# Asking for the third expert's weights as soon as the order of experts is known

## The reference, cut to what matters

```python
def moe_ffn(h, router_w, router_bias, w_gate, w_up, w_down):
    ...
    _, idx = lax.top_k(jnp.where(in_group, sel, -jnp.inf), TOP_K)
    ...
    for e in range(N_EXPERTS):
        he = jax.nn.silu(h @ w_gate[e]) * (h @ w_up[e])
        y = y + gates[..., e:e + 1] * (he @ w_down[e])
    return y
```

## Time and profile before

| | |
|---|---|
| median of 3 runs | 1428.83 us |
| lowest and highest | 1424.74, 1430.57 us |
| profiled execution | 1431.29 us |
| its span, first to last instruction | 1429.5 us |
| granted tensor engine clock, mean | 0.881 of full |
| PE busy | 1155.3 us (81%) |
| DVE busy | 459.9 us (32%) |
| ACT busy | 265.1 us (19%) |
| DMA moved | 344.03 MB, mean 241 GB/s |

### The profile page before, as it was taken

How to read it: one execution, slowest core, us unless ns; L and a number is a source line. 1 busy time by engine, 2 the same in 40 slices (tenths; PEclk the granted TensorE clock), 3 DMA queues, 4 the chain that set the end, 5 groups by cost and what they waited for, 6 DMA issues and landing times.

```text
span 1429.5 us, 15764 instructions
## 1 busy us (share of the span) xinstructions
PE 1155.3 (81%) x5976; PEld 566.9 (40%) x5976; DVE 459.9 (32%) x1107; ACT 265.1 (19%) x588; POOL 122.2 (9%) x107
## 2 busy tenths in 40 slices
PE   4899978888989469999895499977799399985554
PEld 1363433444654223333332347533478233322223
DVE  2321355764742601111111511356762401110013
ACT  1320101223520401111111412100241211100002
POOL 2000031820000100000000200034100100000001
PEclk8899999979899779999998699997579699997776
DMA  9612106739995489999999410005001599999972
GB/s 347 227 64 113 59 0 241 297 132 413 375 354 209 166 311 381 393 396 389 394 418 400 171 51 9 0 23 213 0 1 59 202 374 383 397 410 416 426 322 92
DMA packets 86997, 344.03 MB, mean 241 GB/s; under 512 B 6918, under 2 KB 42187, under 8 KB 64395
## 3 DMA queue, kind: packets, MB, share of 16 engines
q1 hardware_dynamic: 67056, 308.76, 55.6%
q10 hardware_dynamic: 15867, 20.77, 4.3%
q0 software_dynamic: 4000, 13.49, 2.6%
HBM read 300.92 MB, written 42.07 MB: 240 GB/s over the span
## 4 chain that ended last, share of the span: by engine, by line
PE 64%; DMA 17%; DVE 11%; ACT 3%; issue 2%; POOL 1%; ACTq 1%; SPq 1%; POOLq 0%; DVEq 0%
PE ps L888 15%; PE ps L502 12%; DMA ring<-in_exp_w_up 10%; PE ps L911 7%; PE ps L790 6%; PE ps L511 5%; PE ps L445 4%; DMA ring<-in_w_mod 3%; PE ps L467 3%; DMA arena<-in_exp_w_up 2%; PE ps L769 2%; PE ps L687 2%; PE ps L667 2%; PE ps L739 1%; DMA arena<-slots,slot_ids 1%
## 5 line engine op out<-in xcount | busy, mean ns | idle before, releaser
L888 PE MATMUL ps<-ring,arena 128*32 128x256 f32 (+1 forms) x1344 | 198.7, 532 | 44.0 <-DMA ring<-in_exp_w_up 44.0
L445 PE MATMUL ps<-cst,arena 128*128 128x128 f32 x558 | 100.6, 311 | 95.9 <-DMA arena<-slots 37.2
L502 PE MATMUL ps<-u,ring 128*128 128x512 f32 (+1 forms) x416 | 166.9, 561 | 9.8 <-ACT u L1729 4.0
L1587 DVE TENSOR_TENSOR arena<-arena,ps 128x128 f32<-128x128 f32 (+1 forms) x59 | 27.0, 499 | 379.3 <-ACT arena L1885 379.3
L445 PEld LDWEIGHTS ps<-cst,arena 128*128 128x128 f32 x558 | 69.7, 158 | 177.2 <-issue 58.4
L888 PEld LDWEIGHTS ps<-ring,arena 128*32 128x32 f32 (+1 forms) x1344 | 70.6, 136 | 155.2 <-issue 114.7
L502 PEld LDWEIGHTS ps<-u,ring 128*128 128x128 f32 x416 | 79.6, 193 | 94.6 <-issue 89.6
L888 PE MATMUL ps<-arena 128*64 128x512 f32 (+1 forms) x544 | 84.1, 536 | 24.6 <-DMA arena<-in_exp_w_up 24.6
L911 PE MATMUL ps<-arena 128*32 128x256 f32 (+1 forms) x672 | 93.4, 482 | 1.6 <-ACT arena L1894 1.6
L790 PE MATMUL ps<-u,ring 128*128 128x512 f32 (+1 forms) x256 | 85.3, 495 | 2.3 <-DVE h L1421 1.3
L511 PE MATMUL ps<-ring,u 128*128 128x256 f32 (+1 forms) x224 | 76.6, 502 | 7.7 <-DVE arena L1240 7.7
(11 more groups left out here) (285 smaller groups left out, 1203.3 us busy)
## 6 DMA issues: line engine op xcount, KB each, us to landing
ring<-in_w_mod SPq DMA_DIRECT2D x24, 2048.0 KB, 11.6
ring<-in_exp_w_gate SPq DMA_DIRECT2D x22, 2048.0 KB, 23.3
ring<-in_exp_w_up SPq DMA_DIRECT2D x22, 2048.0 KB, 27.0
arena<-in_exp_w_down SPq DMA_DIRECT2D x22, 2048.0 KB, 21.3
slots<-zeros SPq DMA_DIRECT2D x4, 6144.0 KB, 42.5
arena<-in_exp_w_gate SPq DMA_DIRECT2D x10, 2048.0 KB, 24.0
arena<-in_exp_w_up SPq DMA_DIRECT2D x10, 2048.0 KB, 29.5
u<-in_exp_w_down SPq DMA_DIRECT2D x10, 2048.0 KB, 26.5
```

Of the source, the lines that this page charges most:

```text
L445: return nc.tensor.transpose(dst, src, ident[0:n, 0:n])
L502: last = nc.tensor.matmul(bank[row:row + width, 0:T - c0], w[:, k, n:n + width], u[:, k, c0:T], start=(k == 0), stop=(k == KT - 1))
L888: last = nc.tensor.matmul(ps[n * part:n * part + n, 2 + b % 2, 0:2 * width].rearrange("p (s n) -> p s n", s=2), x_k, pair[:, :, a:a + widt ...
```

## The change

After the wait for the order and the passes, gate and up of place 2 are asked for at once. Then SyncE waits for `ut_taken` and asks for down of place 2. Then it waits for the scatter and asks for down of place 1. The wait for block 1's rows (`x_landed1`) is gone. From place 3 on nothing changes.

```diff
                     sp.wait_ge(S("order_ready"), l + 1)
                     sp.wait_ge(S("passes_ready"), l + 1)
-                    sp.wait_ge(S("scattered", l), 32 * (TT - FIRST_T[l]))
-                    sp.wait_ge(S("x_landed1", l), 16 * (P // expert_blocks(l)[1][3]))
                     nc.sync.reg_load(passes_left, passes[0:1, l:l + 1])
                     nc.sync.reg_add(passes_left, passes_left, 1)
-                    load_down(1, 1)
                     for o, r in list(enumerate(rank_order(l)))[FIXED:]:
                         e = nc.sync.value_load(order[0:1, r:r + 1], min_val=0, max_val=NE - 1)
                         load_gate_up(o, e)
+                        if o == FIXED:
+                            sp.wait_ge(S("ut_taken"), ut_count(l, TT - 1, 1) + 1)
                         load_down(o, e)
+                        if o == FIXED:
+                            sp.wait_ge(S("scattered", l), 32 * (TT - FIRST_T[l]))
+                            load_down(1, 1)
```

## The result

The changed kernel takes 1457.47 us (median of 4 runs, 1453.31 to 1459.85) against 1429.7 us for the kernel before in the same comparison: ratio 1.0187, 95% interval 1.0163 to 1.0211. It is 27.8 us slower by the medians, 26.7 by the ratio, which isn't their quotient. The forecast was 1439 with a range from 1427 to 1446: the side was right, the size was not.

The account below looks back on a forecast made before the run. Both expert stages were taken to end when the last weights land, with DMA engines full and later asks waiting for the tensor engine. Layer 0 +13.4 and layer 1 -3.3 gave +10.1 us on the 1428.83 median: 1439, range 1427 to 1446.

Parts of the forecast that it names:

- the turns that the scatter waits: Weight packets sent ahead of remaining scatter packets on each DMA engine: scatter 13.3 us later in layer 0, 3.8 in layer 1.
- the tokens: Token loads of blocks 0 and 1 meeting queued weights: 3.2 us more in layer 0, 9.7 for 3.4 in layer 1.
- the slack of the start: Layer 0: second token pair landed 1.2 us before its transpose, so 1.2 us was taken off the start's delay.
- the stock: Queued weight loads covering a late tensor engine at the thinnest ask: 1.9 us in layer 0, 10.5 in layer 1.
- a start more than 20 us late in layer 0: Last listed case, the tensor engine starting over 20 us late in layer 0; chance 0.05.
- the ceiling of the gain: Most the early asks could bring: 1.9 us in layer 0 plus 4.8 in layer 1, 6.7 us.
- marks named in the prediction: Expected profile signs: asks near 498 and 1132, scatter wait ending near 521 and 1139.5, layer 0's last load 13 us later.
- the ratio of 1.67 packets of the scatter for one of the weights: DMA engine sharing, from 157 software queue packets beside 94 of q1: 49 scatter packets let 29 weight turns pass.
- Case C: Rival, scatter and weight packets one for one: +15.1 us in layer 0, +12.5 together, 1441; chance 0.55 shared with the forecast.
- the prediction's own row of two hardware queues: Over 4 us q1 moved 79 packets of 16 KB, q10 80 of 2 KB: one for one, whatever the size.
- rival B: Scatter passes in bulk, nine packets a turn: +6.1 us in layer 0, -4.8 in layer 1, 1430; chance 0.30.
- its upper case: All 15 us of weights pass before the scatter: layer 0 start +17.0, end +15.1; up to 1446 with extra costs.

Follow-up runs that it names:

- x9: Kernel before with 45 small ScalarE copies ahead of its first token copy in each layer, so only the tensor engine starts later: +14.2 us, ratio 1.0111.
- x1: Changed kernel, but SyncE waits for the scatter before gate and up of place 2: +4.7 us against the kernel before, ratio 1.0034.
- x2: Of the change only place 2's gate load goes early; the other loads wait for scatter and tokens: +8.7 us against the kernel before, ratio 1.0054.
- x3: Changed kernel with gate and up of place 2 as four strided loads each, in 2 KB packets: +11.8 us against the kernel before, ratio 1.0081.
- x4: Changed kernel with the wait for block 1's rows put back ahead of down 1 alone: +19.7 us against the kernel before, ratio 1.0134.
- x5: Kernel before without SyncE's wait for block 1's rows, nothing ahead of the scatter: +6.6 us, ratio 1.0025 (0.9998 to 1.0053).
- x7: The change in layer 1 alone, layer 0 as in the kernel before: +5.3 us against the kernel before, ratio 1.0037.

## Why the prediction was wrong

**The steps that failed, in short.** The path was right: weights ahead of the scatter, a late scatter, late tokens, a late start, a late end of layer 0. Four terms of its sum were mis-sized, all to the same side: the turns that the scatter waits (13.3 us, measured 15.8), the tokens (3.2 and 6.3, measured 4.9 and 9.1), the slack of the start (1.2, measured 0.1) and the stock (1.9 and 10.5, measured none and 6.5). In layer 1 they turned the sign: forecast 3.3 us earlier, measured 4.4 later. The case that came, a start more than 20 us late in layer 0, had been given a chance of 0.05.

**The bound and the direction.** That the stages end with the last weights, that the asks after place 2 hang on the tensor engine's start, that the ceiling of the gain is small and that the early asks would pay for it by a late start: all hold. x9 shows the second by itself, x1 and x2 the last. Of the marks named in the prediction two are there: asks 2 us after the passes, DMA share below 1 behind the start. The others, the scatter's landing, the first product and the ends of both stages, came later than named.

**The turns of the scatter, 13.3 us in layer 0 and 3.8 in layer 1.** Measured 15.8 and 6.4 (11.5 us after the passes in place of 5.1). The step that failed is the ratio of 1.67 packets of the scatter for one of the weights, taken from the gathers beside 2 KB packets at the end of a weight load (790 to 792). It was not a property of two full queues. The same trace of the kernel before, 788 to 790 and 794 to 796:

```profile
q1 hardware_dynamic: 359, 0.73, 98.0%
q0 software_dynamic: 13, 0.05, 6.7%
...
q0 software_dynamic: 204, 0.74, 92.6%
q1 hardware_dynamic: 40, 0.08, 10.2%
```

The weight load was running out, so 1.67 was one point on the way from 13 for 359 to 204 for 40. Beside 16 KB packets the ratio is 1.0, beside the 2 KB packets of x3 it is 0.57. Case C, one for one, with 15.0 us, was nearest, and the prediction's own row of two hardware queues, 79 to 80, pointed to it. The Trainium skill (DMA: Bandwidth & Descriptors, Queues, rings and completion order) has each engine go round its queues packet by packet, with some 9 to 17 descriptors in a typical packet. The counts agree with the round and rule out rival B, nine of the scatter for one of the weights: they are 185 beside 182. Equal counts can't tell one for one from nine for nine, but the rate does. In x4, 506 to 516, 40 slices of 0.25 us:

```profile
GB/s 442 475 377 311 639 328 279 508 508 213 524 557 344 557 229 197 656 639 66 541 721 49 541 590 180 541 590 180 524 639 115 492 705 98 475 737 147 672 311 98
```

From the middle on it has its lowest value in every third slice, so it repeats each 0.75 us. One weight packet took 0.62 us and one of the scatter 0.16, estimates from the shares and bytes of the queues under x4; nine of each would take 7 us. Here single recorded packets took turns, and a turn was as long as its packet; that a whole group of 9 to 17 goes at a turn is not borne out.

**The tokens, +3.2 us in layer 0 and +6.3 in layer 1 from first packet to landing of block 1.** Measured from scatter to landing of block 1: 10.2 in place of 5.3 us in layer 0 (+4.9), 14.2 in place of 5.1 in layer 1 (+9.1). From the first token packet to the landing of block 1 it was 5.6 in place of 3.6 us in layer 0 (+1.9, less than forecast) and 10.1 in place of 3.4 in layer 1 (+6.7). The rest is the late first packet behind a weight ask, 2.9 us in layer 0 and 2.4 in layer 1, which no term of the sum had.

**The start.** 15.8 + 4.9 = 20.7, measured 20.6 in layer 0 (forecast 15.3). The 1.2 us of slack that I took off were not to be had: between the landing of block 1 and its transpose lie the transpose and ScalarE's copy of block 0. In the kernel before that copy (513.36) waited for ScalarE's own eight token asks, which ended at 513.2; in the changed kernel block 0 itself landed at 536.7, 0.8 us ahead of block 1, and its copy came at 538.00 and the transpose of block 1 at 538.64. In layer 1 the start was 12.8 us late (forecast 7.2): 6.4 of scatter, 9.1 of tokens less 2.8 that block 1's rows had waited there before and now did not (transpose 2.9 us after their landing at 1140.7, now 0.1 after 1179.9).

**The stock, 1.9 us in layer 0 and 10.5 in layer 1.** This is the largest miss of a single term in layer 1, 4.0 us. I had measured the idle queue on loads with no token traffic beside them: 7.7 us for a down load. In the stage the block loads and stores go on. The same ask that was read in the earlier trace rows with 9.6 us took this on a queue that was all but empty in the changed kernel (asked at 595.50, KB, us to landing):

```profile
arena<-in_exp_w_down SPq DMA_DIRECT2D x1, 2048.0 KB, 10.3
```

So layer 0 had no stock at all at that ask, 9.6 against 10.3, and E equals D to 0.3 us. x9 shows 1.3 us there, within the scatter, and 12.5 - 6.0 = 6.5 in layer 1; x5, without early asks ahead of the scatter too, 8.5 - 2.1 = 6.4. With D = 12.8, x9's layer 1 would be some 6.3 us longer; the change's is 4.4, and x7's, the same code with D = 13.0, 5.6. So the idle time that the early asks used gave back 2 us in the one profile and 0.9 in the other, which single profiles don't tell from nothing. That the stage's other traffic is what made the reading on an idle queue too good is argued and wasn't tried; the size of the stock is measured by x9.

**The sum by the measured terms.** Layer 0: +20.6 - 0 = +20.6, seen +20.9, forecast +13.4. Layer 1: +12.8 - 6.5 = +6.3, seen +4.4, forecast -3.3; the 1.9 us between stay open. Of the 15 us between the stages' 25.3 and the forecast's 10.1, 7.5 are in layer 0 (5.3 of start, 2.2 of stock) and 7.7 in layer 1 (5.6 of start, the rest of stock). With the 3.2 us outside the stages these are the 18.4 us by which the profiled execution, 1459.8, missed the 1441.4 forecast on its clock. The range ended at 1446 because its upper case moved only the scatter's turns, with some 5 us added for closing packets and the restart; the tokens and the stock had been given one value each. That was the second error: three terms came from rows of other stretches and only one had both ends.

## What to carry to other kernels

Before asking for a large load early, ask which small transfers are on the critical path at that moment: here the queues shared a DMA engine by packets, so a 4 KB packet of 0.16 us waited behind a 16 KB one of 0.62 us, four times its own length, and filling the DMA engines is then a loss although their share says idle. When the buffers are few, count the stream from the event that frees them: an earlier ask for what fits now buys nothing beyond the stock, and a later start of the consumer delays all that follows. Read a ratio of two queues from a stretch in which both are full from end to end, and the stock of a queue against loads that have the stage's other traffic beside them.

## What the runs showed of the hardware

- Recorded packets of two loaded queues went one for one with 16 KB weight packets beside 4 KB scatter packets (182 to 185, 224 to 222), but 1008 to 576 with 2 KB packets beside the scatter. Gathers beside a weight load that ran out went 157 to 94, then 204 to 40. A single ratio for a queue is not to be had.
- A token load asked for behind or within 0.13 us of a weight load of another queue moved its first packet 3.6 to 4.3 us after its ask (eight stages), without such a load 1.3 to 1.4 us (twelve stages). The cause wasn't tried by itself.
- Strided asks were dear for the engine that issues them: SyncE needed 3.3 us and 7.0 us for the four asks of gate and of up in layer 0 of x3, 3.2 and 3.4 us in layer 1, 0.35 us for one whole load. Why up took twice as long in layer 0 is open.
